# Moving five of nine modulation rounds from a feed-forward layer into the gaps of an attention

## What is computed

```
c_act = silu(c);  c_ctx_act = silu(c_ctx)
mx = split(c_act @ w_mod[l] + b_mod[l], 9)       # for the tokens
mc = split(c_ctx_act @ w_mod[l] + b_mod[l], 9)   # for the context
x = x + 0.5 * mx[2] * swiglu(modulate(rms_norm(x), mx[0], mx[1]), ...)
```

## Time and profile before

| | |
|---|---|
| runs | 2594.11, 2595.48, 2589.21 us; median 2594.11 |
| the profiled execution | 2593.96 us, span 2592.2 us |
| TensorE matmul, weight load busy | 2492.9 us (96%), 2162.4 us (83%) |
| VectorE, ScalarE busy | 1344.4 us (52%), 1035.4 us (40%) |
| DMA | 372.28 MB, mean 144 GB/s |
| mean granted TensorE clock | 0.986 |
| first layer's modulation | chunk matmuls from 20.4 to 316.2 us |
| second layer's modulation | chunk matmuls from 520.7 to 742.7 us |
| first attention, scores of its first to last pair | 1251.1 to 1354.8 us |

### The profile page before, as it was taken

One profiled execution on the slowest core, in us unless ns is written; L12 is line 12 of the kernel. 1 busy time (PEld: TensorE's weight loads), 2 busy tenths in 40 slices (PEclk: granted clock), 3 DMA queues, 4 the chain that ended last, 5 costly groups with the idle time before them and its releaser, 6 DMA issues. The chain is left out here.

```text
span 2592.2 us, 37237 instructions
## 1 busy us (share of the span) xinstructions
PE 2492.9 (96%) x15710; PEld 2162.4 (83%) x15710; DVE 1344.4 (52%) x2230; ACT 1035.4 (40%) x1660; POOL 0.2 (0%) x4
## 2 busy tenths in 40 slices
PE   7999999999999999999789999999999998988999
PEld 6998789988998888888567888888888887878999
DVE  6657454655453334357886433335333347846553
ACT  5534544444433223146563322214222216743443
POOL 0000000000000000000000000000000000000000
PEclk9999999999999999999999999999999999998999
DMA  9886733488862333335102333332333326502564
GB/s 326 285 276 211 233 128 98 135 328 303 315 213 90 98 98 98 97 115 185 51 1 66 98 98 98 98 96 90 95 97 95 97 90 177 182 16 66 174 184 147
DMA packets 146727, 372.28 MB, mean 144 GB/s; under 512 B 20330, under 2 KB 67074, under 8 KB 146562
## 3 DMA queue, kind: packets, MB, share of 16 engines
q1 hardware_dynamic: 146274, 369.59, 44.6%
q10 hardware_dynamic: 288, 0.31, 0.1%
HBM read 368.71 MB, written 1.15 MB: 143 GB/s over the span
## 5 line engine op out<-in xcount | busy, mean ns | idle before, releaser
L298 DVE TENSOR_TENSOR weights_lo<-weights_raw,weights_hi 128x1024 fp32r<-128x1024 f32 (+2 forms) x547 | 658.0, 1212 | 489.1 <-ACT weights_hi L292 485.8
L350 PE MATMUL psum<-normed_hi,weights_hi 128*128 128x256 f32 (+2 forms) x2664 | 883.4, 332 | 21.3 <-DVE normed_lo L629 6.5
L350 PE MATMUL psum<-normed_lo,weights_hi 128*128 128x256 f32 (+2 forms) x2664 | 869.1, 326 | 0.0
L350 PE MATMUL psum<-normed_hi,weights_lo 128*128 128x256 f32 (+2 forms) x2664 | 868.6, 326 | 0.0
L292 ACT CAST weights_hi<-weights_raw 128x1024 fp32r<-128x1024 f32 (+2 forms) x547 | 562.6, 1035 | 375.8 <-DMA weights_raw<-in_w_down 251.7
L350 PEld LDWEIGHTS psum<-normed_hi,weights_hi 128*128 128x128 f32 (+1 forms) x2664 | 510.8, 192 | 85.5 <-issue 34.9
L350 PEld LDWEIGHTS psum<-normed_lo,weights_hi 128*128 128x128 f32 (+1 forms) x2664 | 512.5, 192 | 40.9 <-issue 1.2
L350 PEld LDWEIGHTS psum<-normed_hi,weights_lo 128*128 128x128 f32 (+1 forms) x2664 | 512.0, 192 | 40.4
L350 PE MATMUL psum<-hidden_hi,weights_hi 128*128 128x512 f32 (+1 forms) x594 | 217.6, 366 | 0.0
L350 PE MATMUL psum<-hidden_hi,weights_lo 128*128 128x512 f32 (+1 forms) x594 | 217.1, 365 | 0.0
L350 PE MATMUL psum<-hidden_lo,weights_hi 128*128 128x512 f32 (+1 forms) x594 | 217.0, 365 | 0.0
(11 more groups left out here) (264 smaller groups left out, 2734.1 us busy)
## 6 DMA issues: line engine op xcount, KB each, us to landing
weights_raw<-in_w_gu SPq DMA_DIRECT2D x220, 512.0 KB, 3.7
weights_raw<-in_w_down SPq DMA_DIRECT2D x110, 512.0 KB, 3.6
arena<-in_w_mod SPq DMA_DIRECT2D x72, 512.0 KB, 6.9
weights_raw<-in_w_x SPq DMA_DIRECT2D x24, 512.0 KB, 7.0
resid<-in_w_mod SPq DMA_DIRECT2D x24, 512.0 KB, 7.6
normed_raw<-in_w_mod SPq DMA_DIRECT2D x24, 512.0 KB, 7.5
under_normed_hi<-in_w_mod SPq DMA_DIRECT2D x24, 512.0 KB, 7.7
weights_raw<-in_w_qk SPq DMA_DIRECT2D x24, 512.0 KB, 4.5
```

What stands on the lines that cost most here:

```text
L298: ve.tensor_tensor(w_lo[:, c % RING, a], w_raw[:, c % RING, a], w_hi[:, c % RING, a].bitcast(F32), ALU.subtract).then_inc(lo_ready, 1)
L350: last = te.matmul(out, a, b, start=start and n == 0, stop=stop and n == 2)
```

## The change

The second layer's modulation is cut in two. Rounds 0 to 3 stay in the third segment, spread over the same 0.1 to 0.95. Rounds 4 to 8 become side steps of the first attention. Their ring is six places that are free then: three slots of the rounded weights, the buffer of the norms' squares, and two stretches of the arena. Their sums and turns use bank 7, that of the output turns; so rounds 4, 6 and 8 wait until the turn ahead of them is read out, and later output turns wait until the round ahead is read. In two more edits the first layer's modulation starts at 0.04 of the first segment, not at 0, and the last two parts of the output are placed one step earlier.

```diff
+MOD_EARLY = 4
...
-            def __init__(self, layer, ring, after=None):
-                self.layer, self.ring, self.after = layer, ring, after
-                self.n = MOD_ROUNDS * (KD // 4 + 1) + 1
-                self.first = layer * MOD_ROUNDS
+            def __init__(self, layer, ring, after=(), rounds=(0, MOD_ROUNDS), bank=MOD_BANK, bank_read=()):
+                self.layer, self.ring, self.after, self.bank, self.bank_read = layer, ring, after, bank, bank_read
+                self.rounds, self.complete = rounds[1] - rounds[0], rounds[1] == MOD_ROUNDS
+                self.n = self.rounds * (KD // 4 + 1) + 1
+                self.first = layer * MOD_ROUNDS + rounds[0]
+
+            def read(self, r):
+                return mod_read, self.first + r + 1
...
                     if k == 0 and r > self.first:
                         pe.wait_ge(mod_read, r)
+                    if k == 0 and self.bank_read:
+                        pe.wait_ge(*self.bank_read[r - self.first])
                     for m in range(4):
                         self.chunk(pe, r, k + m)
...
-                if i == self.n - 1:
+                if i == self.n - 1 and self.complete:
                     dve.wait_ge(mod_read, r)
...
-            ([Modulation(0, mod_ring0)], 0, 1),
+            ([Modulation(0, mod_ring0)], 0.04, 1),
...
-            ([Modulation(1, mod_ring1, (a1_max, NT * HG))], 0.1, 0.95),
+            ([Modulation(1, mod_ring1, [(a1_max, NT * HG)], (0, MOD_EARLY))], 0.1, 0.95),
...
+        c = len(chunk_at)
+        late_ring = [under_w_hi[:, (c + n) % RING, :].rearrange("p (a n) -> p a n", a=4) for n in range(LEAD, RING)]
+        late_ring += [squares.rearrange("p a (b n) -> p (a b) n", n=MOD_W), at(24088, 4, MOD_W), at(15872, 4, MOD_W)]
+        late_mod = Modulation(1, late_ring, [(used, c), heads.done(15)], (MOD_EARLY, MOD_ROUNDS), TURN_BANK,
+                              [out_turns.done(n) for n in (1, 1, 3, 3, 5)])
+        for n, r in ((2, 1), (4, 3), (6, 4)):
+            out_items[n].needs.append(late_mod.read(r))
+        m_steps = steps_of(late_mod)
...
+        mod_places = (7, 12, 13, 14, 15, 16, 17, 20, 21, 22, 23, 24, 25, 28, 30, 32)
+        side = sorted([*side, *zip(mod_places, m_steps)], key=lambda placed: placed[0])
         in_order(beside(steps_of(attend), side, per=2))
...
-        side = [((b * KF - 1) // CT + 2, step) for (_, b), step in zip(Output.parts, output)]
+        side = [((b * KF - 1) // CT + (2 if b < 7 else 1), step) for (_, b), step in zip(Output.parts, output)]
```

More of the change, by code:

```diff
@@ L204, in build @@
         w_raw, w_hi, w_lo = raw_hi_lo("weights", RING, SLOT)
+        under_w_hi = nc.alloc_sbuf_tensor_at("under_weights_hi", [P, RING, SLOT], F32, offset=hi_at["weights"])
         normed_raw, *normed = raw_hi_lo("normed", KD, 2 * S)
@@ L792, in load @@
             def load(self, sp, m):
-                if m < MOD_ROUNDS * KD:
+                if m < self.rounds * KD:
                     c = self.first * KD + m
@@ L801, in sync @@
                 if i == 0:
-                    if self.after:
-                        sp.wait_ge(*self.after)
+                    for event in self.after:
+                        sp.wait_ge(*event)
                     for m in range(MOD_RING):
@@ L818, in tensor @@
                     for b in range(MOD_W // P):
-                        last = te.transpose(psum[:, MOD_BANK, MOD_W + b * P:MOD_W + (b + 1) * P],
+                        last = te.transpose(psum[:, self.bank, MOD_W + b * P:MOD_W + (b + 1) * P],
                                             mod_rows_sb[:, (r - 1) % 2, b * P:(b + 1) * P], ident)
@@ L831, in chunk @@
                 for g in range(4):
-                    last = te.matmul(psum[32 * g:32 * g + 32, MOD_BANK, 0:MOD_W], cond[:, k, :],
+                    last = te.matmul(psum[32 * g:32 * g + 32, self.bank, 0:MOD_W], cond[:, k, :],
                                      self.ring[c % MOD_RING][:, g, :],
@@ L842, in scalar @@
                         act.wait_ge(mod_turned, r - 1)
-                    se.copy(mod_rows_sb[:, r % 2, :], psum[:, MOD_BANK, 0:MOD_W]).then_inc(mod_rows, 1)
+                    se.copy(mod_rows_sb[:, r % 2, :], psum[:, self.bank, 0:MOD_W]).then_inc(mod_rows, 1)
             def vector(self, dve, step, i):
@@ L851, in vector @@
                     new = mod[:, m:m + 4 * nb, :].rearrange("p (g b) s -> p b g s", b=nb)
-                    src = psum[:, MOD_BANK, MOD_W:2 * MOD_W].rearrange("p (b g s) -> p b g s", b=nb, g=4)[:, :, :, 0:2]
+                    src = psum[:, self.bank, MOD_W:2 * MOD_W].rearrange("p (b g s) -> p b g s", b=nb, g=4)[:, :, :, 0:2]
                     bias = col("b_mod", m, 4 * nb).rearrange("p (g b o) -> p b g o", b=nb, o=1)
                     ve.tensor_tensor(new, src, bias.to_broadcast([P, nb, 4, 2]), ALU.add).then_inc(mod_read, 1)
-                if i == self.n - 1:
+                if i == self.n - 1 and self.complete:
                     dve.wait_ge(mod_read, r)
```

## The result

The changed kernel takes 2602.26 us (median of 8 runs, 2597.62 to 2607.22), the kernel before, beside it, 2594.53: a ratio of 1.0034 with an interval of 1.0024 to 1.0044. It is slower by 0.34%, 8.8 us; a second series of runs gave 1.0027 (1.0016 to 1.0038). The forecast was 0.8 us faster, and the range ended at 2600.5.

What follows compares the result with a forecast made beforehand. TensorE was taken as full in the first feed-forward layer, TensorE and VectorE as both near full in the first attention. Terms -21.4 + 24.4 - 3.8 + 0 = -0.8 us gave 2593.3 us, range 2582.5 to 2600.5.

Steps and rivals of the forecast that it cites:

- The layer that gives: First feed-forward layer: TensorE is the limit, so removing five rounds takes off their work and a load wait, -21.4 us.
- The attention that takes: First attention: five added rounds cost +24.4 us, from their work, bank waits, loads and VectorE, less waits filled.
- Two turns no longer stand back to back, the norm comes later: First attention: the load-only step pushes one earlier turn and the first output norm back, -0.5 us, bounds -1 and +2.
- The bank wait: First attention: three late rounds wait for the output turn ahead to be read from the shared bank, +5.6 us, bounds 0 and 7.
- the 3.0 us absorbed: First attention: TensorE's waits for VectorE of 0.67 and 2.28 us are filled by modulation work, -3.0 us; the others stay.
- The landing: First attention: late loads of 512 KB land in 3.5 us with the DMA idle, so waits cost +0.7 us, bounds 0 and 9.
- The second rival: First attention: loads land late, 7.7 us each, so waits cost 12.9 us instead of 0.7, giving 2605.5 us, slower; chance 0.10.
- The start: First 40 us: later modulation loads remove 3.0 us of waits and 1.7 of slow clock, add 0.9: -3.8 us.
- The 1.7 us for the clock: From 30 to 40 us: work lost at granted clock 0.83, right after the modulation-load wait, expected to go.
- the third rival: First 40 us: the later modulation start gives nothing, its waits only come later: 2597.1 us, no change; chance 0.13.
- The end: Output: turning the fourth part ahead of the last chunk changes nothing, zero us, bounds -0.5 and +0.3.
- The first rival: First attention swallows the rounds: 6.0 us of waits filled, no bank or load waits, giving 2584.0 us; chance 0.20.

Runs made afterwards that it cites:

- the earlier turn: The changed kernel with each group's second output turn behind base step 11 instead of 12: 2592.95 us, ratio 0.9993 to the kernel before.
- the output as before: The changed kernel with load step at place 6, second output turns one step earlier, and the output's last two parts at their old places: 2589.42 us, ratio 0.9988.
- The kernel before with the earlier turn: The kernel before with only each group's second output turn behind base step 11 instead of 12: 2597.12 us, ratio 1.0006.
- both edits: The changed kernel with the late rounds' load step at place 6 instead of 7 and each second output turn one step earlier: 2589.90 us, ratio 0.9986.
- the rounds left out: The changed kernel without its five late rounds, their loads, products and turns; those vectors are the bias alone: 2572.45 us, ratio 0.9922 to the kernel before.

## Why the prediction was wrong, point by point

**The layer that gives** was right: 21.2 us in the trace for 21.4.

**The attention that takes** was 3 to 5 us short: 27.2 to 29.1 by the runs (some 4 us either way), for 24.4. Two of its steps failed.

- "Two turns no longer stand back to back, the norm comes later: an estimate of -0.5, bounds -1 and +2." It counted the shift as time and did not ask what would be in front of the norm on VectorE. The answer is base step 10's work, 3.1 us, and TensorE reaches pair 11 2.7 to 3.2 us later. The sign was wrong, and the bound by that reading too; the runs alone (1.6 to 3.4 us, and 3.05 beside the earlier turn, with overlapping intervals) don't tell it from 2.
- The bank wait's length was right (6.5 for 5.6, under the bound of 7), its price was not: 8.8 to 10.95 us by the runs. A stall was costed at its own length. It also left some of VectorE's delay unfilled that a chunk step in another place would have filled, and was in part followed by steps at half clock. The rule of the Trainium skill's "Perfetto Trace Analysis", section Matmuls, that independent groups should rotate through PSUM banks, was weighed at 5.6 us; the trace agrees with it, at 1.6 to 2 times that price. No run gave all five rounds a bank of their own.

The clock is no third step of this kind. The prediction set nothing for it in the attention, and the two profiles of the changed kernel, at granted clocks of 0.87 and 0.93 there, differ by 3.9 us. But 0.93 is what it was before, and in that second profile the attention is still 28.3 us longer than before.

Of the rest, the 3.0 us absorbed were right: the waits of 0.67 and 2.28 are gone from the profile, and the others stayed (1.26, 1.22). The landing was right by luck: 0.6 us in the first profile for 0.7, but 2.1 in the second, and a load takes 6 us, not 3.5. "The DMA is idle here" was true of other work, not of the rounds' own chunks. The second rival had the landing time nearly right, but not its price of 12.9 us: the largest sum of such waits in the runs read here is 4.8 us (the output as before).

**The start** was 3.8 us too good: "Both should go." Of the 3.0 us of waits, 2.8 came back: 1.3 us for the convolution's weights (0.9 was set for that) and 1.5 for later modulation loads, one of them at 31 us, where none was expected. The 1.7 us for the clock rested on one execution. The kernel before with the earlier turn has the same start and the same 3.1 us of waits there, and its granted clock from 30 to 40 us is 1.00, not 0.83. In the changed kernel it is 0.83 from 20 to 30 us in the first profile (matmuls of 256 columns from 21.59 us on come 0.21 us apart instead of 0.12) and 1.00 in the second. This is the third rival; it was given 0.13 and happened.

**The end** was right: nothing.

So the halves missed on the same side: what gives was counted 5.0 us too high (25.2 with the start, against 20.2, interval 16.9 to 23.9), what takes 2.8 to 4.7 too low. The three failed terms come to more than that together, some 10 to 13 us against 9.6 (7 to 12 by the interval); the difference is within the noise of the runs. The slower outcome came through terms that stood in the sum with a wrong price, not through the rival that ended on that side.

The first rival did not come true in the changed kernel, but part of it may with both edits. There the five rounds cost 0.9986 - 0.9922, 16.6 us (some 4 us either way), against the 20.2 us of their own work that was priced in the layer that gives: less, but not clear of the noise. What shows in the profiles is that chunk steps stand where TensorE would wait: it waits 5.4 us for VectorE's L1759 in the attention with both edits, and 9.3 for the same step with the rounds left out. The Trainium skill's "Perfetto Trace Analysis", section Optimization Strategy, says that interleaving regimes may improve performance; here one order of the same steps lost 0.34%, and another gained 0.14%.

## What to carry to other kernels

When a step is slipped into a hand-written order, ask for every step that it pushes back what will be ahead of it on each engine's queue, not only how much later it comes; a place further back can be a whole iteration of another engine. A new stall on the busiest engine can cost more than its length, so move the producer of the stalled resource one iteration earlier before accepting the stall: here one place was worth 9 to 11 us for 6.5 us of stalls and turned a loss of 0.3% into no change, and with the norm back in its place into a gain of 0.1%. Work moved into gaps pays where TensorE waits for something already on its way. Before a term of a few us is read off a profile, look at the same stretch in a second one: here two executions of one kernel differ by 3.9 us in one stretch.

## What was not expected of the hardware

- Two profiles of one kernel with the same four long waits differ by 3.9 us in the attention, with stretches at half clock behind different waits. Behind the bank wait of 2.04 us at 1322.81 one ran 24 matmuls in 2.79 us, the other in 1.50. Why one wait and not the other is left open.
- Loads of 512 KB with hardly any other traffic took 5.3 to 7.7 us, close to the 6.9 and 7.7 of the crowded early stages: a chunk step frees its slots in groups, and within one such group the landing times rose from 3.4 to 6.5 us.
